# Gate and up products of six feed-forward blocks by seven products on 2x2x2 blocks, with the down product in pieces between them

## The reference

```python
# first kind, x [512, 1024], w_gate and w_up [1024, 2816], w_down [2816, 1024]
f = (jax.nn.silu(x @ w_gate[l]) * (x @ w_up[l])) @ w_down[l]
x = _layernorm(ALPHA * x + f, ln2_g[l], ln2_b[l])
# second kind
x = h + 0.5 * swiglu(rms_norm(h, ffn2_norm[l]), ffn2_gate[l], ffn2_up[l], ffn2_down[l])
```

## Time and profile before

| | |
|---|---|
| median of 3 runs | 3143.33 us (3143.02 to 3143.93) |
| span of the profiled execution | 3141.2 us |
| PE busy | 3116.4 us (99%), 15518 matmuls |
| weight loads (PEld) | 2588.2 us (82%) |
| DVE busy | 1147.4 us (37%) |
| ACT busy | 713.8 us (23%) |
| POOL busy | 2259.0 us (72%) |
| DMA | 284.07 MB, mean 90 GB/s |

### The profile page before, as it was taken

One profiled execution on the slowest core, in us unless ns is written; L12 is line 12 of the kernel. 1 busy time (PEld: TensorE's weight loads), 2 busy tenths in 40 slices (PEclk: granted clock), 3 DMA queues, 4 the chain that ended last, 5 costly groups with the idle time before them and its releaser, 6 DMA issues.

```text
span 3141.2 us, 44673 instructions
## 1 busy us (share of the span) xinstructions
PE 3116.4 (99%) x15518; PEld 2588.2 (82%) x15518; DVE 1147.4 (37%) x1874; ACT 713.8 (23%) x1474; POOL 2259.0 (72%) x3079
## 2 busy tenths in 40 slices
PE   8999999999999999999999999999999999999999
PEld 7879888898798888888887788888888887788887
DVE  5575111275751112632226542212222136542211
ACT  4453110054531100411112321110211022321100
POOL 5347877673468776788777398887888777398884
PEclk9999999999999999999999999999999999999999
DMA  5112322231123222232232132223222232132222
GB/s 185 48 41 86 109 93 95 93 108 42 47 88 104 96 95 90 84 102 98 95 112 92 41 101 95 98 95 100 94 94 100 94 111 88 41 108 94 100 94 68
DMA packets 83017, 284.07 MB, mean 90 GB/s; under 512 B 9531, under 2 KB 15068, under 8 KB 82652
## 3 DMA queue, kind: packets, MB, share of 16 engines
q1 hardware_dynamic: 77484, 273.70, 26.2%
q10 hardware_dynamic: 5424, 8.79, 0.8%
HBM read 278.79 MB, written 3.67 MB: 90 GB/s over the span
## 4 chain that ended last, share of the span: by engine, by line
PE 97%; DVE 2%; ACT 1%; issue 0%; DMA 0%; DVEq 0%; ACTq 0%
PE bank_v L537 21%; PE bank_v L539 20%; PE bank_v L538 20%; PE bank_a L537 9%; PE bank_a L539 9%; PE bank_a L538 9%; PE bank_v L881 1%; PE bank_a L860 1%; PE bank_s L1021 1%; PE bank_s L899 1%; PE bank_v L1036 1%; PE bank_s L591 0%; PE bank_s L1024 0%; PE bank_a L584 0%; PE bank_s L889 0%; PE bank_s L907 0%
## 5 line engine op out<-in xcount | busy, mean ns | idle before, releaser
L511 POOL TENSOR_TENSOR w_lo<-raw,w_hi 128x512 fp32r<-128x512 f32 x1024 | 1414.7, 1382 | 81.8
L508 POOL TENSOR_TENSOR zero<-zero 128x1 f32<-128x1 f32 x1024 | 277.3, 271 | 769.0 <-PE bank_v L539 578.8
L537 PE MATMUL bank_v<-xn_hi,w_hi 128*128 128x512 f32 (+1 forms) x1680 | 640.9, 381 | 8.1 <-DVE xn_lo L1700 8.0
L509 POOL CAST w_hi<-raw 128x512 fp32r<-128x512 f32 x1024 | 639.1, 624 | 0.0
L539 PE MATMUL bank_v<-xn_hi,w_lo 128*128 128x512 f32 (+1 forms) x1680 | 635.0, 378 | 0.0
L538 PE MATMUL bank_v<-xn_lo,w_hi 128*128 128x512 f32 (+1 forms) x1680 | 634.6, 378 | 0.0
L537 PE MATMUL bank_a<-xn_hi,w_hi 128*128 128x512 f32 (+1 forms) x1232 | 469.0, 381 | 2.3 <-ACT work L1248 1.4
L539 PE MATMUL bank_a<-xn_hi,w_lo 128*128 128x512 f32 (+1 forms) x1232 | 466.7, 379 | 0.0
L538 PE MATMUL bank_a<-xn_lo,w_hi 128*128 128x512 f32 (+1 forms) x1232 | 466.6, 379 | 0.0
L537 PE MATMUL bank_v<-h_hi,w_hi 128*128 128x512 f32 (+1 forms) x1122 | 422.9, 377 | 0.0
L538 PE MATMUL bank_v<-h_lo,w_hi 128*128 128x512 f32 (+1 forms) x1122 | 422.4, 376 | 0.0
(11 more groups left out here) (357 smaller groups left out, 3114.5 us busy)
## 6 DMA issues: line engine op xcount, KB each, us to landing
raw<-in_w_stream SPq DMA_DIRECT2D x516, 512.0 KB, 3.3
rope<-in_rope ACTq DMA_DIRECT2D x2, 1024.0 KB, 5.7
da_v<-t_rows ACTq DMA_DIRECT2D x2, 1024.0 KB, 6.5
out<-resid SPq DMA_DIRECT2D x8, 256.0 KB, 2.3
t_rows<-t_row ACTq DMA_DIRECT2D x1, 1536.0 KB, 7.4
resid<-in_x ACTq DMA_DIRECT2D x5, 256.0 KB, 7.2
mla_v<-in_alibi ACTq DMA_DIRECT2D x2, 512.0 KB, 7.5
resid<-in_x SPq DMA_DIRECT2D x3, 256.0 KB, 9.4
```

Source lines behind the costliest of these rows:

```text
L508: pool.tensor_tensor(zero[:, 1:2], zero[:, 0:1], zero[:, 0:1], ALU.add)
L509: pool.tensor_copy(w_hi[:, u, cut], raw[:, u, cut]).then_inc(*hi_split.done(("unit", u, n)))
L511: ins = pool.tensor_tensor(w_lo[:, u, cut], raw[:, u, cut], w_hi[:, u, cut].bitcast(F32), ALU.subtract)
L537: pe.matmul(out, lhs_hi, rhs_hi, start=first, stop=False)
```

## The change

Two neighbouring hidden chunks (a "quad", weight columns 1 and 2), the two halves of the 1024 input features and the two halves of the 512 tokens make 2x2x2 blocks. For the first two quads of a block (four chunks) nothing changes; for the other nine, gate and up are each a step, 18 steps per block. In a step the eight block products are replaced by seven (Winograd's form of Strassen's), each of four 128-deep tiles, three matmuls per tile, 256 columns wide. From the weights come four sums: S1 = A21 + A22, S2 = S1 - A11, S3 = A11 - A21, S4 = A12 - S2, on POOL (`weight_sums`); ACT and DVE split A11, A12, A22 and the sums into high and low parts in a ring of seven places. From x come four sums T1 to T4, once per block, on DVE, split likewise; in layer2 x times its gain is first copied to `x_gained` by ACT.

Partial results are accumulated in three banks of a step (a, b, e from `bank_a` and `bank_s`); ACT copies bank a three times in between (t1, u2, u4), and DVE joins a copy with another bank for the quarters 11, 21 and 22. Between the seven products of a step PE runs two parts of the down product, four tiles each, on chunks of h that are ready: `PARTS` are 37 parts, added to `resid` by DVE one by one; what is left, two tiles for five output chunks and six for three, is `down_tail`. So h needs six places instead of 22, and the unit stream is reordered: two gate or up units and one down unit per step. `LN_HALVED` for ln2 becomes 6, as for ln1 (two output chunks in halves), and both use one starting order. The loops of all engines are written out, and POOL's add to `zero` is gone.

The diff, cut to its core. Constants:

```diff
+QUADS = FC // 2
+OPEN_QUADS = 2
+STEPS = 2 * (QUADS - OPEN_QUADS)
+RING = dict(A11=0, A12=1, S3=2, S2=3, S1=4, S4=5, A22=6)
...
+H_SLOTS = 6
+PARTS = ([(n, range(4 * g, 4 * g + 4)) for g in range(4) for n in range(DC)]
+         + [(n, range(16, 20)) for n in range(5)])
+TAIL_CHUNKS = [range(20 if c < 5 else 16, FC) for c in range(DC)]
...
-LN_HALVED = dict(ln1=DC - 2, ln2=DC - 1)
+LN_HALVED = dict(ln1=DC - 2, ln2=DC - 2)
```

SP's waits ahead of a load, and POOL:

```diff
+                left = STREAM_UNITS[n - SLOTS]
+                if left is None:
+                    sp.wait_ge(w_split.sem, w_split.credit + PLAIN[n - SLOTS] + 1)
+                else:
+                    layer, l, tag, s, second = left
+                    with counts.within(layer, l):
+                        sp.wait_ge(*s_lo.after((tag, s, "A22" if second else "A")))
+                        sp.wait_ge(*s_sum.after((tag, s, "S4")))
...
-                        pool.tensor_tensor(zero[:, 1:2], zero[:, 0:1], zero[:, 0:1], ALU.add)
...
+            def weight_sums(n, tag, s):
...
+                pool.wait_ge(*w_used.after((tag, "gate1", 0)))
+                if s:
+                    pool.wait_ge(*s_lo.after((tag, s - 1, "S14")))
+                pool.wait_ge(*raw_in[n % SLOTS].after(("unit", n)))
+                pool.wait_ge(*raw_in[(n + 1) % SLOTS].after(("unit", n + 1)))
+                sum_pair((tag, s, "S1"), s1, a21, a22, ALU.add)
+                sum_pair((tag, s, "S3"), s3, a11, a21, ALU.subtract)
+                pool.wait_ge(*s_sum.after((tag, s, "S1")))
+                sum_pair((tag, s, "S2"), s2, s1, a11, ALU.subtract)
+                pool.wait_ge(*s_sum.after((tag, s, "S2")))
+                sum_pair((tag, s, "S4"), s4, a12, s2, ALU.subtract)
```

PE's steps:

```diff
+            def ffn_steps(tag):
+
+                pe.wait_ge(*a_read.after((tag, "gate1", 1)))
+                for s in range(STEPS):
+                    a, b, e = quad_banks(s)
+                    pe.wait_ge(*s_lo.after((tag, s, "A")))
+                    quad_product((tag, s, "P1"), a, "A11", *x_quarter(0, HALVES[0]), True)
+                    quad_product((tag, s, "P2"), e, "A12", *x_quarter(1, HALVES[0]), True)
+                    pe.wait_ge(*s_lo.after((tag, s, "S32")))
+                    pe.wait_ge(*x_lo.after((tag, "T")))
+                    quad_product((tag, s, "P7"), b, "S3", *x_sum(3), True)
+                    pe.wait_ge(*snap.after((tag, s, "t1")))
+                    quad_product((tag, s, "P6"), a, "S2", *x_sum(2), False)
+                    down_part(tag, 2 * s)
+                    pe.wait_ge(*s_lo.after((tag, s, "S14")))
+                    pe.wait_ge(*snap.after((tag, s, "u2")))
+                    quad_product((tag, s, "P5"), a, "S1", *x_sum(1), False)
+                    down_part(tag, 2 * s + 1)
+                    pe.wait_ge(*snap.after((tag, s, "u4")))
+                    quad_product((tag, s, "P3"), a, "S4", *x_quarter(1, HALVES[1]), False)
+                    pe.wait_ge(*s_lo.after((tag, s, "A22")))
+                    pe.wait_ge(*quad.after((tag, s, "22")))
+                    quad_product((tag, s, "P4"), b, "A22", *x_sum(4), False)
```

ACT, the opening of a scaled block and the beginning of a step:

```diff
+                act.wait_ge(*w_used.after((tag, "gate0", 0)))
+                for c in range(DC):
+                    act.activation(x_gained[:, c, :], resid[:, c, :], ACT.Copy, scale=par2[:, column + c:column + c + 1]
+                                   ).then_inc(*x_full.done((tag, c)))
+                root(stats, 1)
+                if early:
+                    x_sums_high(tag)
+                hidden(0, 0)
+                if not early:
+                    x_sums_high(tag)
+                hidden(0, 1)
+                hi_a(tag, 0)
+                hidden(1, 0)
+                hi_s32(tag, 0)
+                hi_s14(tag, 0)
+                hi_a22(tag, 0)
+                hidden(1, 1)
+                ffn_steps(tag, True)
...
+            def ffn_steps(tag, is_scaled):
+
+                for s in range(STEPS):
+                    if s:
+                        hi_s14(tag, s)
+                        hi_a22(tag, s)
+                    take_snap(tag, s, 0, "t1", "P1")
+                    if s:
+                        second_out(tag, s - 1, is_scaled)
+                    if s + 1 < STEPS:
+                        hi_a(tag, s + 1)
+                    if s % 2 == 0:
+                        ready = (value if is_scaled else quad).after((tag, s, "11"))
+                        gate_silu(tag, s, "11", ready, work[:, 0, HALVES[0]], work[:, 0, HALVES[0]])
+                    if s:
+                        act.wait_ge(*quad.after((tag, s - 1, "21")))
+                    take_snap(tag, s, 1, "u2", "P6")
+                    if s + 1 < STEPS:
+                        hi_s32(tag, s + 1)
+                    take_snap(tag, s, 2, "u4", "P5")
+                    if s % 2:
+                        h_high(tag, 2 * (s // 2 + OPEN_QUADS), work[:, 2, :])
+                    elif is_scaled:
+                        gate_silu(tag, s, "12", value.after((tag, s, "12")), work[:, 0, HALVES[1]], work[:, 0, HALVES[1]])
...
```

DVE's steps:

```diff
+            def ffn_steps(tag, is_scaled, part_out):
+
+                for s in range(STEPS):
+                    a, b, e = quad_banks(s)
+                    gate, chunk = s % 2 == 0, 2 * (s // 2 + OPEN_QUADS)
+                    own = work[:, 0 if gate else 2, :]
+                    if s:
+                        second_out(tag, s - 1, is_scaled)
+                        lo_s14(tag, s)
+                        lo_a22(tag, s)
+                        if gate:
+                            h_low(tag, chunk - 1, work[:, 3, :])
+                    if not gate and is_scaled:
+                        gate_again(tag, s, 0, ("11", "12"))
+                    dve.wait_ge(*snap.after((tag, s, "t1")))
+                    join(tag, s, "11", prod.after((tag, s, "P2")), own[:, HALVES[0]], 0, e)
+                    if not gate:
+                        if is_scaled:
+                            dve.wait_ge(*product.after((tag, s, "gate", 0)))
+                        else:
+                            dve.wait_ge(*gated.after((tag, s - 1, "11")))
+                        dve.tensor_tensor(own[:, HALVES[0]], own[:, HALVES[0]], work[:, 0, HALVES[0]], ALU.mult)
+                        if is_scaled:
+                            gate_again(tag, s, 1, ("2",))
+                    elif is_scaled:
+                        dve.tensor_tensor(own[:, HALVES[0]], own[:, HALVES[0]], scale_by[:, HALVES[0]], ALU.mult
+                                          ).then_inc(*value.done((tag, s, "11")))
+                    if s + 1 < STEPS:
+                        lo_a(tag, s + 1)
+                    part_out(tag, 2 * s)
+                    if s + 1 < STEPS:
+                        lo_s32(tag, s + 1)
+                    join(tag, s, "22", snap.after((tag, s, "u4")), work[:, 1 if gate else 3, HALVES[1]], 2, b)
+                    part_out(tag, 2 * s + 1)
+                    if not gate:
+                        if not is_scaled:
+                            dve.wait_ge(*gated.after((tag, s - 1, "12")))
+                        dve.wait_ge(*prod.after((tag, s, "P3")))
+                        dve.tensor_tensor(own[:, HALVES[1]], a[:, 0:S // 2], work[:, 0, HALVES[1]], ALU.mult
+                                          ).then_inc(*product.done((tag, "h", chunk)))
+                        h_low(tag, chunk, own)
+                    elif is_scaled:
+                        dve.wait_ge(*prod.after((tag, s, "P3")))
+                        dve.tensor_tensor(own[:, HALVES[1]], a[:, 0:S // 2], scale_by[:, HALVES[1]], ALU.mult
+                                          ).then_inc(*value.done((tag, s, "12")))
+                second_out(tag, STEPS - 1, is_scaled)
+                h_low(tag, FC - 1, work[:, 3, :])
+                part_out(tag, len(PARTS) - 1)
```

## The result

The changed kernel takes 3157.32 us (median; 3154.65 to 3158.86), the kernel before 3143.63 us beside it: ratio 1.0043, 95% interval [1.003, 1.0055]. It is slower by 0.43%, where 3121.5 us and faster had been forecast; the time lies within the range given. The profiled execution took 3154.65 us, with a span of 3152.9 us.

A forecast was written before the change was run, and what follows sets the result against it. The prediction took PE to bound the kernel. Span 3141.2 - 87.8 (steps) + 33 (openings) + 30 (ends) + 3 (clock) = 3119.4 us; with 2.1 us from span to median, 3121.5 us; range 3085 to 3170.

The forecast's parts named there:

- What bounds the kernel, and the pitch: PE, busy 99% of the span; 256-column products start every 0.120 us, 512-column every 0.2267; gain 87.8 us.
- The rival without a constant in the pitch: Gate and up steps: half the columns take half the time, gaining 147 us, 3062 us; chance 0.02.
- the smaller constant that the prediction takes from the Trainium skill: Gap between matmuls: constant 2.5 ns instead of 13, by which the 108 steps would gain 128 us.
- The other engines keep the step: Steps of 15.52 us: DVE, POOL and ACT deliver in time, 0 us of PE wait; upper bound 25 us.
- The rival for "slower": Scaled up steps: port shared by DVE and POOL makes join "22" late; 3193 or 3157 us; chance 0.20.
- one of its cases: Scaled pairs of steps: each 1 us longer from the shared port, 3157 us.
- Openings: Ahead of each block's first step: new sums and copies make PE wait 33 us in all, bounds 5 and 52.
- Ends: Down tails: PE waits for evictions behind shorter chunks, 30 us in all, bounds 18 and 42.
- Clock: Behind new PE waits: two more falls to granted clock 0.50, 2.4 us rounded to 3, bounds 0 and 8.
- Smaller delays: 256- and 512-column matmuls starting late at full clock: no term in the prediction, listed as forecast 0.
- The likeliest case: Whole kernel: steps at PE's pitch, openings and ends as forecast, 3100 to 3137 us; chance 0.50.
- The nearest rival: Whole kernel: openings and ends near their upper bounds cancel the gain, 3143.5 us; chance 0.10.

The follow-up runs named there:

- Runs 1 and 2: Changed kernel with PE's wait for both gate1 banks split by bank, 3160.44 us; then also copy t1 ahead of the last opening unit's silu and h_hi, 3148.67 us.
- run 4: Changed kernel with 5 to 27 small ACT copies ahead of t1 in steps 4, 8 and 12 of each block; 3215.25 us in a single execution.
- the third run: Changed kernel whose last step runs no down parts, so three tail chunks are 6 matmuls and five are 18; 3146.25 us.

## Why the prediction was wrong

- **What bounds the kernel, and the pitch: right.** 84 products start every 0.120 us, and the work at this pitch is 88.0 us less where 87.8 stood in the sum. The rival without a constant in the pitch falls with it, and so does the smaller constant that the prediction takes from the Trainium skill (TensorE: Matmul & The Clock Gate, section "Back-to-back issue gap"), which gives it for a single matmul.
- **The other engines keep the step: right.** The walk ended with 0 us of wait per step, and all scaled steps but the first take 15.56 us, like the unscaled ones. The rival for "slower", the shared port as the bound of the scaled steps, did not happen; the kernel got slower by another way. That this rival names 3157 for one of its cases is chance.
- **Openings: 33 forecast, 33.8 measured.** The sum is that near because errors cancel: layer1 8.9 for 12, first ffn1 13.4 for 15, the others 11.6 for 6. The place named (a_read of gate1's second unit, behind hi_s32, hi_s14 and hi_a22) is the line with 21.8 us. Runs 1 and 2 add what the prediction did not see: behind that wait stood t1, h_lo and u2, each nearly as late, so taking away the named one brought nothing.
- **Ends: 30 forecast, 33.4 measured.** Layer2 13.3 for 14, the last block 4.6 for 6.5, layer1 15.5 for 9. There the waits at two chunks (1.7 and 2.8 us) were foreseen in kind; the 3.1 us ahead of the next projection, behind ln2's statistics, was not, and no run tested its cause.
- **Clock: the step that failed.** "With some 20 more waits I take two more falls, 2.4 us, rounded to 3; bounds 0 and 8." The trace has nine more stretches at 0.50 and 50.1 us more of such time, and the table of the span shows 16.7 us of slower starts in the 256- and 512-column products. The price of a fall, 1.2 us from the earlier trace rows, was near: the stretches of 3.4 us cost 1.2 to 1.6 us each. What was wrong is their number, two, for which the sum gives no reason while it held 63 us of waits (there are 32 more waits over 0.4 us), and that several last longer. In run 4 every graded wait from 2.3 us on had its stretch. The first steps of ffn2 and of ffn1's second lap lost 2.6 to 2.8 us each this way (18.2 to 18.4 us instead of 15.56), beside 3.7 to 4.2 us of wait.
- **Smaller delays: a second step that failed, a term put at nothing.** 10.6 us, nearly all in the down product: its 512-column matmuls stand 10.2 us behind their pitch, 0.1 us before. Of this 6.0 us are in the steps, where the first five of the twelve matmuls of a part start 2 to 9 ns late each and the rest on their pitch, and 4.1 us in the tails. The pitch of the earlier trace rows was read in a long run of like products and put on pieces between others. The cause of the delay was not tested and stays open.
- **How the numbers followed.** The terms' errors: -0.2, +5.8, +13.7, +10.6 and +3.6, 33.5 us of span together, more than the 21.8 us that were left of the gain. No one of them turns the sign: with the clock right in the sum 8.1 us of gain would stay, with the smaller delays as well it is 2.5 us of loss. The likeliest case left no room for that: its upper end was 3137. The nearest rival was the third, gain and waits cancel, at 3143.5 and a chance of 0.10; its bounds had the clock at 3, too.

## What to carry to other kernels

Price new waits of the tensor engine at their length and at the slower matmuls that go with the long ones: here some 17 us on 69 us of waits, and 13 to 21 us on some 40 us in the fourth run. When an opening is late, write down everything that the first step asks for with its time, since the second- and third-latest wait stand just behind the one that the profile names. Steady steps can gain what their pitch says and the kernel still lose, if the work that was cover for evictions and copies is spread into those steps.

## What the runs showed of the hardware

- In the fourth run's graded waits, a tensor engine that stood still for 2.3 to 4.1 us had 3.4 us at granted clock 0.50 with it, one that stood still for 9.5 us had 10.2 us; eleven waits of up to 1.9 us had none.
- The same wait did not always cost the same: ahead of the first P1 in ffn2 (first lap), 3.7 us of wait went with 6.83 us at 0.50 in the changed kernel, with 3.41 us in the third run and with none in the fourth, and the first step took 18.2, 17.1 and 16.7 us.
- One added wait on GpSimd, which holds four of its operations back, took 11 us off the kernel: DVE's operations of 1024 elements in x_sums_low went from a median of 2.03 us to 1.22 us.
